# A 32-expert mixture layer whose experts are taken in an order computed on the chip

## What is computed

```
for every expert e, on the tokens that chose it:
    hu = x[toks] @ w_up[e] + b_up[e]            # 1024 x 2048, 8 MB
    y  = clamped_swiglu(hu) @ w_down[e] + b_down[e]   # 1024 x 1024, 4 MB
    out[toks] += gate * y
```

## Time and profile before

| | |
|---|---|
| time, median of 3 | 1395.23 us (1394.46 to 1398.86) |
| the profiled execution, its own time | 1392.76 us |
| its span, first to last instruction | 1391.0 us |
| mean granted TensorE clock | 0.938 of full |
| TensorE busy | 1186.3 us, 85% |
| VectorE, ScalarE busy | 22%, 18% |
| weights and inputs read | 463.22 MB, mean 334 GB/s |

### The profile page before, as it was taken

One profiled execution on the slowest core, in us unless ns is written; L12 is line 12 of the kernel. 1 busy time (PEld: TensorE's weight loads), 2 busy tenths in 40 slices (PEclk: granted clock), 3 DMA queues, 4 the chain that ended last, 5 costly groups with the idle time before them and its releaser, 6 DMA issues.

```text
span 1391.0 us, 20661 instructions
## 1 busy us (share of the span) xinstructions
PE 1186.3 (85%) x7931; PEld 582.3 (42%) x7932; DVE 309.0 (22%) x783; ACT 253.2 (18%) x370; POOL 0.2 (0%) x4
## 2 busy tenths in 40 slices
PE   4999899987977899998678777877787889799996
PEld 2745588835332334243234332333333333434432
DVE  1125454264111122121112111111111112103213
ACT  3035422112012111112111112111112020200211
POOL 0000000000000000000000000000000000000000
PEclk9999999997999999999899889987899999799998
DMA  9942475353779999989999999999999999955890
GB/s 335 380 154 90 177 262 212 137 213 152 278 267 419 416 417 418 418 356 420 418 416 417 418 418 418 418 418 416 417 419 418 418 418 417 415 198 181 337 415 34
DMA packets 102361, 464.79 MB, mean 334 GB/s; under 512 B 8124, under 2 KB 9364, under 8 KB 69430
## 3 DMA queue, kind: packets, MB, share of 16 engines
q1 hardware_dynamic: 100368, 461.52, 83.1%
q10 hardware_dynamic: 1958, 2.78, 0.6%
HBM read 463.22 MB, written 1.05 MB: 334 GB/s over the span
## 4 chain that ended last, share of the span: by engine, by line
PE 39%; DMA 19%; SPq 13%; issue 3%; DVE 2%; ACT 0%; DVEq 0%
PE psum L876 17%; DMA ring<-in_w_up 14%; PE psum L949 10%; SPq L485 7%; PE psum L826 6%; SPq L480 6%; DMA ring<-in_w_down 5%; PE psum L868 2%; PE psum L967 2%; DVE area L1540 1%; PE psum L912 1%; PE psum L851 1%; DVE area L1525 1%; PE psum L817 0%; DVE area L1563 0%
## 5 line engine op out<-in xcount | busy, mean ns | idle before, releaser
L876 PE MATMUL psum<-ring,area 128*32 128x512 f32 (+2 forms) x2432 | 413.1, 649 | 77.1 <-DMA ring<-in_w_up 77.0
L876 PEld LDWEIGHTS psum<-ring,area 128*32 128x32 f32 (+2 forms) x2432 | 101.9, 123 | 375.7 <-issue 227.6
L949 PE MATMUL psum<-ring,area 128*32 128x256 f32 (+1 forms) x2080 | 199.0, 422 | 26.5 <-DVE area L1525 14.8
L826 PEld LDWEIGHTS psum<-area 128*128 128x128 f32 x1056 | 131.4, 206 | 35.1 <-issue 35.1
L826 PE MATMUL psum<-area 128*128 128x128 f32 x1056 | 138.0, 292 | 0.3 <-DVE area L1470 0.3
L949 PEld LDWEIGHTS psum<-ring,area 128*32 128x32 f32 (+1 forms) x2080 | 71.7, 114 | 143.2 <-issue 79.6
L1500 DVE TENSOR_SCALAR area<-psum 128x256 f32<-128x256 f32 x51 | 21.6, 424 | 453.8 <-PE psum L876 453.8
L1138 ACT ACTIVATE area<-area 128x256 f32<-128x256 f32 x51 | 21.3, 417 | 443.3 <-DVE area L1500 443.3
L1126 ACT ACT_TABLE_LOAD x32 | 41.1, 1283 | 327.8 <-PE psum L851 327.8
L525 PE MATMUL psum<-hT,ring 128*128 128x256 f32 x370 | 83.6, 386 | 0.0
L525 PE MATMUL psum<-ring,hT 128*128 128x512 f32 (+1 forms) x192 | 77.8, 561 | 0.0
(11 more groups left out here) (177 smaller groups left out, 666.4 us busy)
## 6 DMA issues: line engine op xcount, KB each, us to landing
ring<-in_w_up SPq DMA_DIRECT2D x256, 1024.0 KB, 19.3
ring<-in_w_down SPq DMA_DIRECT2D x128, 1024.0 KB, 22.7
ring<-in_ada_w SPq DMA_DIRECT2D x12, 2048.0 KB, 16.6
ring<-in_w_in SPq DMA_DIRECT2D x11, 2048.0 KB, 19.6
ring<-in_w_out SPq DMA_DIRECT2D x2, 2048.0 KB, 10.2
ring<-in_w_branch_b SPq DMA_DIRECT2D x1, 2048.0 KB, 9.6
cst<-in_cst ACTq DMA_DIRECT2D x1, 1168.0 KB, 9.4
x_res<-in_x SPq DMA_DIRECT2D x1, 1024.0 KB, 5.1
```

What stands on the lines that cost most here:

```text
L826: ins = pe.matmul(ps[banks[i]][:, kk % 4 * P:(kk % 4 + 1) * P], h2[:, tt, kk * P:(kk + 1) * P], S[:, tt, 0:P], start=(tt == 0 and kk % 4 = ...
L876: ins = pe.matmul(ps[b][g * P // G:(g + 1) * P // G, 0:w], XT[:, kk, t0:t0 + P // G], wt[:, c0:c0 + w], start=False, stop=kk == KT - 1, sk ...
L949: ins = pe.matmul(ps[b][g * M:(g + 1) * M, 0:w], hidT[:, p, q * P + of * M:q * P + (of + 1) * M], down_weights(kk)[:, g * W + d * CW:g * W ...
```

## The change

Expert 0 stays first. The other 31 are ranked by token count, most first (ties by number), and put at positions by a fixed table, `rank_at`: rank r+2 goes to position 1 + (3r + 5) mod 31, so ranks 2, 3, 4, ... go to positions 6, 9, 12, ... The list of expert numbers and the list of their classes are computed by VectorE (12 small operations) with one product on TensorE, and are written to `order_i`. Every engine, SP included, then reads number and class of position e from this list. `cls_i` is kept for expert 0 alone.

```diff
+def rank_at():
+    ranks = np.ones(E)
+    for r in range(E - 1):
+        ranks[1 + (3 * r + 5) % (E - 1)] = r + 2
+    return ranks
...
-        cls_i = sb("cls_i", E + 1, I32)
+        cls_i = sb("cls_i", 1, I32)
+        order_i = sb("order_i", 2 * (E + 1), I32)
...
+        def expert_at(eng, e):
+            return eng.value_load(order_i[0:1, ds(e, 1)], min_val=0, max_val=E - 1)
+
+        def class_at(eng, e):
+            return eng.value_load(order_i[0:1, ds(E + 1 + e, 1)], min_val=0, max_val=NC - 1)
...
+            sp.wait_ge(order_ready, 1)
             with sp.Fori(1, E) as e:
+                number = expert_at(sp, e)
...
-                    up_load(e, kk)
+                    up_load(number, kk)
...
-                    down_load(e, j)
+                    down_load(number, j)
...
-            pe.wait_ge(cls_ready, 1)
...
             gathers(FIRST_BANKS, 0)
             gathers(FIRST_BANKS, 1)
+            pe.wait_ge(place_ready, 1)
+            place = lg[0:E, 3, 0:E]
+            fill("order", [(ps[6][0:1, 0:E], cst[0:E, C_NUM:C_NUM + 1], place, True, True),
+                           (ps[6][0:1, E:2 * E], lg[0:E, 1, 2:3], place, True, True)])
+            pe.wait_ge(order_ready, 1)
...
-            act.wait_ge(cls_ready, 1)
             for i in range(2):
                 act.wait_ge(xg_full, i + 1)
                 tokens_out(FIRST_BANKS, i)
+            act.wait_ge(order_ready, 1)
...
+            count, key, own = lg[:, 5, 0:E], lg[:, 7, 0:E], lg[0:E, 0, 0:E]
+            number_id = ident[0:E, 0:E]
+            key_col, rank, class_col = (lg[0:E, 1, i:i + 1] for i in range(3))
+            link(v.scalar_tensor_tensor(out=key, in0=iota[:, 0:E], scalar=-1.0 / E, in1=count, op0=ALU.mult, op1=ALU.add))
+            link(v.memset(key[:, 0:1], 2.0 * T))
+            link(v.tensor_tensor(own, key[0:E, :], number_id, ALU.mult))
+            link(v.tensor_reduce(key_col, own, AX_X, ALU.add))
+            link(v.tensor_scalar(own, key[0:E, :], key_col, None, ALU.is_ge))
+            link(v.tensor_reduce(rank, own, AX_X, ALU.add))
+            link(v.tensor_tensor(own, lg[0:E, 6, 0:E], number_id, ALU.mult))
+            v.tensor_scalar(lg[0:E, 3, 0:E], cst[0:E, C_RANK:C_RANK + E], rank, None, ALU.is_equal)
+            v.tensor_reduce(class_col, own, AX_X, ALU.add).then_inc(place_ready, 1)
+            link(v.memset(order_i[:, :], 0))
+            un.wait_full(v, "order")
+            v.tensor_copy(order_i[0:1, 0:E], ps[6][0:1, 0:E])
+            v.tensor_copy(order_i[0:1, E + 1:2 * E + 1], ps[6][0:1, E:2 * E]).then_inc(order_ready, 1)
+            v.wait_ge(order_ready, 1)
...
             def expert(e, root):
-                cls = v.value_load(cls_i[0:1, ds(e, 1)])
+                number, cls = expert_at(v, e), class_at(v, e)
                 v.wait_ge(xg_full, 2 * e + 1)
-                v.tensor_copy(pick, ident[:, ds(e * 4, 4)].rearrange("p (c m) -> p c m", m=1).broadcast_to(
+                v.tensor_copy(pick, ident[:, ds(number * 4, 4)].rearrange("p (c m) -> p c m", m=1).broadcast_to(
...
-                following = v.value_load(cls_i[0:1, ds(e + 1, 1)])
-                return [by_class(v, following, lambda k: one_hot(e + 1, k), "hot", root),
+                following, its_class = expert_at(v, e + 1), class_at(v, e + 1)
+                return [by_class(v, its_class, lambda k: one_hot(following, k), "hot", root),
                         by_class(v, cls, lambda k: body(e, k), "dve", root)]
```

More of the change, by code:

```diff
@@ L102 @@
 C_STACK = C_I64 + P
-C_W = C_STACK + E
+C_RANK = C_STACK + E
+C_NUM = C_RANK + E
+C_W = C_NUM + 1
 R_ADAB, R_G = 0, 48
@@ L135, in constants @@
     c[:, C_STACK:C_STACK + E] = i[:, None] % E == np.arange(E)[None, :]
-    return c
+    c[:, C_RANK:C_RANK + E] = rank_at()
+    c[0:E, C_NUM] = np.arange(E)
+    return c
+def rank_at():
[3 more added lines that the diff above has]
+    return ranks
 def two_pi_parts():
@@ L201, in layer_kernel @@
         pos_i = sb("pos_i", TT, I32)
-        small_rows = sb("small_rows", P, rows=R_N)
         b_router_sb = sb("b_router_sb", E, rows=1)
-        cls_i = sb("cls_i", E + 1, I32)
+        cls_i = sb("cls_i", 1, I32)
+        order_i = sb("order_i", 2 * (E + 1), I32)
         xn = area[:, 0:TT * D]
         arena = area[:, TT * D:]
+        small_rows = arena[0:R_N, 14592:14592 + P]
         ident = cst[:, C_ID:C_ID + P]
@@ L297, in layer_kernel @@
             "cls_ready", "s_ready", "g_ready", "sg_ready"))
+        place_ready, order_ready = sem("place_ready"), sem("order_ready")
         m_ready, act_ready, acc_done, out_ready, stored = map(sem, (
@@ L398, in layer_kernel @@
             un.add(f"acc{b}", b)
+        un.add("order", 6)
         released = {}
@@ L970, in body @@
                 ins.then_inc(acc_done, 1)
-            experts(pe, "pe", lambda e, root: [by_class(pe, pe.value_load(cls_i[0:1, ds(e, 1)]), lambda k: body(e, k), "pe", root)])
+            experts(pe, "pe", lambda e, root: [by_class(pe, class_at(pe, e), lambda k: body(e, k), "pe", root)])
         @block.scalar
@@ L1144, in _ @@
             experts(act, "act",
-                    lambda e, root: [by_class(act, act.value_load(cls_i[0:1, ds(e, 1)]), lambda k: body(e, k), "act", root)])
+                    lambda e, root: [by_class(act, class_at(act, e), lambda k: body(e, k), "act", root)])
             act.wait_ge(acc_done, E + 1)
@@ L1457, in _ @@
                                             in1=lg[:, 6, 0:E], op0=ALU.is_ge, op1=ALU.add))
-            v.tensor_copy(cls_i[:, :], lg[:, 6, 0:E + 1]).then_inc(cls_ready, 1)
+            v.tensor_copy(cls_i[:, :], lg[:, 6, 0:1]).then_inc(cls_ready, 1)
             gate_rows(2, gain2)
```

## The result

The changed kernel takes **1380.88 us** (median of 14, 1377.07 to 1392.04), the kernel before, run beside it 14 times, 1395.2 (1392.08 to 1400.21). The ratio is **0.990, 95% interval 0.9885 to 0.9916**: faster by 14.3 us, where 28 were forecast, and outside the range of 1359 to 1378. The profiled execution took 1379.52 us with a span of 1377.7, against 1391.0 before.

A forecast was written before the change was run, and what follows sets the result against it. The weight stream bounds the expert loop, except where TensorE's work stops it. The terms ended the last expert at 1349.8 instead of 1377.9; these 28.1 us off 1395.23 gave 1367 (70%), range 1359 to 1378.

The forecast's parts named there:

- Step 1: Start to the last tile landing of position 2: 434.07 as before plus 1.2 us for the start, 435.3.
- a fetch like the 5.04: Start of the loop: most the later class read could add, like the 5.04 us ahead of expert 1; 0.9 was taken.
- Steps 2 and 3: Positions 3 to 5 at 30.12 us each, to 525.6; then class 4 entered after 7.01 of issue, at 535.4.
- Step 4: Positions 6 to 8, class 4 and two class 0 experts behind it: 118.8 us, last tile at 654.2.
- Step 5: Positions 9 to 31 at the stream's pace: 23 x 30.12 = 692.8 us, last tile at 1347.0.
- The sign that the prediction named for being wrong: Ahead of the first transpose (L851): issue time over 2 us at ordinary class changes would show the forecast wrong.
- Step 6: After the last tile a class 0 expert needs 2.8 us, ending at 1349.8 instead of 1377.9.
- B: Loop over experts: class 2 spaced by three is too tight, 4.3 us lost at each of four; 1384, 10%.
- C: Start of the loop: it costs more, a fetch of 5.04 us behind the new wait; 1371, 6%.
- D: Entry into class 4: made without its 7.01 us of issue, its body fetched early; 1360, 7%.
- E: Loop over experts: each change of class fetches code, stalling TensorE by 6.1 us more; 1404, 4%.
- F: Whole loop: the order is not in effect, ranks all off or the list as before; 1396, 3%.

The follow-up runs named there:

- the experiment: The changed kernel with its list worked out the same way but experts in the old order: 1408.05 us, ratio 1.0082 against the kernel before.

## Why the prediction was wrong

**What bounds the kernel:** right. The stream's pace of 30.12 us was met exactly in 17 experts in a row, and its 418 GB/s over 28 experts without class 4.

**Step 1, the start: the step that failed first.** The sum took 1.2 us and reasoned that "the read of the class now begins behind the copies"; it costed the copies and not what the early read had been hiding. The up product started 6.7 us later: 4.0 more issue and 2.2 for the bias at the lower clock were the bulk. The upper bound, "a fetch like the 5.04", was the right row and was put aside, and it had no term for the clock after the pause. By the experiment the whole machinery cost 13.9 us. The two profiled executions lie 15.8 apart at the end of the last scatter: some 7 at this place, some 2 in the entries of experts where TensorE leads, and 7 of lower clock, 2.9 in the mixer, 2.5 in expert 26 and 1.6 in expert 31. Whether these last 7 belong to the change is the part left open.

**Steps 2 and 3:** the pace held, and class 4 was entered after 7.40 of issue, 7.01 having been taken: 1.3 off, with gathers at the lower clock ahead of it.

**Step 4:** class 4 itself took 84.5 us for 83.8.

**Step 5, the stream at pace from position 9: wrong up to position 14,** by 7.9 us; this step had no term for a fetch behind class 4. Position 9 took 54.3 us instead of 48.0, since the return to the near body waited 7.18 for code, and 10 and 11 took 21.8 and 21.6 instead of 19.0. TensorE, still late from class 4, could not absorb that before position 14. The kernel before could not show this return: there the class 2 expert three behind class 4 was the last expert. The sign that the prediction named for being wrong, over 2 us of issue at an ordinary change, is what came.

**Step 6, the tail:** right. From the last wait for a tile to the end of the scatter are 3.5 us (2.8 forecast; the scatter ran at 1.89 for 1.15), and the tail of class 2 is gone.

**The order's own worth,** 29.3 in the sum (28.1 + 1.2), measured 27.2. That it came so near is in part luck: step 5 lost 7.9, while the old order, with the machinery in place, became slower inside its loop too: from the first transpose to the end of the last scatter 1043.9 us instead of 1035.0, of which 2.7 belong to the start and 6.2 do not, 4.1 of these being lower clock in experts 26 and 31.

**The rivals.** B, spacing too tight: refuted by the run without class 4. C, the start costs more, was in its kind the truth, but had 6%, and its 4 us more were 5.5. D was not met. E, each change of class fetching code, is wrong as put, but three changes of 21 do stall TensorE for code: into position 1 (5.44), into class 4 (7.40) and out of position 9 (7.18). The Trainium skill ("Runtime: NRT & Kernel Launch", Instruction fetch mechanics) says that a taken branch outside the fetched window waits for its code. Where TensorE paused, the trace agrees: each of these three pauses holds a packet of the instruction queue. The prediction read the short later entries as speaking against the rule; from 780 to 1360 us the class changes 13 times without a packet, so the bodies of classes 0, 1 and 2 were held together. What is dropped when class 4 comes, no run here shows. F: the order took effect.

## What to carry to other kernels

An engine that reads a branch's condition early hides the fetch of the code behind the work still in its queue; before a wait is put ahead of such a read, look for what the old gap was hiding, and add the lower clock of the first matmuls behind the new one. A pause for code is cheap where the engine leads its loads and dear where it lags, so rare bodies belong where slack follows, and where the last piece of work has no fetch ahead of it. To price a change that brings both a mechanism and an order, run the mechanism with the old order: 13.9 against 27.2 us told in one run what the sum of 14.3 hid.

## What was not expected of the hardware

- Entering a body costs at most 1.7 us of issue where its code is held and 4.7 to 9.3 where it is not, and which it is depends on the bodies visited before: the return behind class 4 was short (1.71), the one after the next far body was 7.18, 6.16 or 6.01 in three orders.
- Leaving three unused bodies out of the spanned code took one of these pauses away and moved another (8.39).
- After 6.30 us of issue 16 bias matmuls took 5.15 us, after 2.35 us of issue 2.93; but after 2.23 us, behind gathers at a granted clock of 0.54, 4.60.
